# One loop over the chunks of a layer, with weight buffers chosen by a table, and the first chunk's weights split ahead of its rows

## The reference

```
gates = group_limited_router(x2d, w_router, router_bias)      # top 2 of 16 experts, weights sum to 1
for e in range(16):
    he = silu(x2d @ w_gate[e]) * (x2d @ w_up[e])              # 1024 -> 512
    y = y + gates[:, e:e+1] * (he @ w_down[e])                # 512 -> 1024
x = layer_norm(alpha * x + y)
```

## Time and profile before

| | us |
|---|---|
| median of 3 runs | 1079.57 (1076.26 to 1080.86) |
| the profiled execution | 1080.69 |
| its span, first to last instruction | 1078.9 |
| TensorE busy | 988.3 (92%) |
| VectorE, ScalarE, GpSimd busy | 808.8, 654.7, 546.2 |
| mean granted TensorE clock, 1 is full | 0.959 |
| HBM traffic over the span | 266 GB/s |

### The profile page before, as it was taken

How to read it: one execution, slowest core, us unless ns; L and a number is a source line. 1 busy time by engine, 2 the same in 40 slices (tenths; PEclk the granted TensorE clock), 3 DMA queues, 4 the chain that set the end, 5 groups by cost and what they waited for, 6 DMA issues and landing times.

```text
span 1078.9 us, 15494 instructions
## 1 busy us (share of the span) xinstructions
PE 988.3 (92%) x4852; PEld 793.1 (74%) x4852; DVE 808.8 (75%) x963; ACT 654.7 (61%) x733; POOL 546.2 (51%) x292
## 2 busy tenths in 40 slices
PE   5997999499999999999988988994999999999995
PEld 4875777377888788887667767783788888888882
DVE  2997757687878777777877977377777778787876
ACT  4324722367878787877513337412787878788861
POOL 3535354065656565645325364441556565656553
PEclk9999999689999999999989989996899999999998
DMA  8625183489999999994813211643899999999962
GB/s 287 198 78 204 40 299 137 138 312 349 359 346 363 360 338 340 346 360 158 259 41 107 89 48 40 228 181 125 289 366 349 376 358 356 367 353 335 366 226 84
DMA packets 122256, 268.51 MB, mean 249 GB/s; under 512 B 10475, under 2 KB 25995, under 8 KB 121712
## 3 DMA queue, kind: packets, MB, share of 16 engines
q1 hardware_dynamic: 111088, 247.14, 63.3%
q0 software_dynamic: 11136, 20.96, 7.3%
HBM read 259.19 MB, written 27.79 MB: 266 GB/s over the span
## 4 chain that ended last, share of the span: by engine, by line
PE 65%; DVE 22%; issue 4%; POOL 3%; DMA 2%; ACT 2%; DVEq 1%; SPq 0%; POOLq 0%; ACTq 0%
PE bank L763 32%; PE bank L781 17%; PE bank L424 7%; DVE bank L1155 7%; PE bank L741 2%; POOL xtok L1600 2%; PE bank L564 1%; DVE xTl L1124 1%; PE bank L735 1%; DVE moemem L1411 1%; DVE w_gate L1131 1%; DVE small L1119 1%; DMA w_gate<-in_w_in 1%; DMA y_rows<-moemem,scatter_idx 1%; DVE wl L1124 1%
## 5 line engine op out<-in xcount | busy, mean ns | idle before, releaser
L1649 POOL TENSOR_TENSOR wl<-w_down,wh 128x2048 fp32r<-128x2048 f32 x33 | 151.8, 4599 | 148.7 <-ACT wh L1023 148.7
L1124 DVE TENSOR_TENSOR wl<-w_gate,wh 128x2048 fp32r<-128x2048 f32 x71 | 166.8, 2349 | 48.3 <-ACT wh L1023 29.4
L1124 DVE TENSOR_TENSOR wl<-w_up,wh 128x2048 fp32r<-128x2048 f32 x66 | 151.2, 2293 | 29.5 <-ACT wh L1023 28.7
L1023 ACT ACTIVATE wh<-w_down 128x2048 fp32r<-128x2048 f32 x66 | 126.8, 1920 | 30.8 <-PE bank L763 30.2
L1023 ACT ACTIVATE wh<-w_up 128x2048 fp32r<-128x2048 f32 x66 | 126.5, 1917 | 31.0 <-PE bank L781 23.3
L763 PE MATMUL bank<-wh,xTl 128*128 128x512 f32 x528 | 144.0, 395 | 1.4 <-DVE xTl L1124 1.4
L763 PE MATMUL bank<-wl,xTh 128*128 128x512 f32 x528 | 143.6, 394 | 1.6 <-DVE wl L1124 1.6
L763 PE MATMUL bank<-wh,xTh 128*128 128x512 f32 x528 | 144.6, 397 | 0.2 <-ACT wh L1023 0.2
L1586 POOL TENSOR_TENSOR wl<-w_gate,wh 128x2048 fp32r<-128x2048 f32 x17 | 78.2, 4602 | 130.4 <-ACT wh L880 130.0
L1023 ACT ACTIVATE wh<-w_gate 128x2048 fp32r<-128x2048 f32 x66 | 126.5, 1917 | 11.0 <-PE bank L781 7.5
L1124 DVE TENSOR_TENSOR xTl<-bank,xTh 128x512 fp32r<-128x512 f32 (+1 forms) x168 | 89.6, 573 | 51.9 <-issue 24.7
(11 more groups left out here) (225 smaller groups left out, 1802.8 us busy)
## 6 DMA issues: line engine op xcount, KB each, us to landing
w_up<-in_exp_w_up SPq DMA_DIRECT2D x32, 2048.0 KB, 19.5
w_down<-in_exp_w_down SPq DMA_DIRECT2D x32, 2048.0 KB, 18.6
w_gate<-in_exp_w_gate SPq DMA_DIRECT2D x32, 2048.0 KB
w_gate<-in_w_in SPq DMA_DIRECT2D x14, 1024.0 KB, 5.4
w_gate<-in_w_out SPq DMA_DIRECT2D x8, 1024.0 KB, 5.0
y_rows<-moemem SPq DMA_DIRECT2D x8, 512.0 KB, 9.5
x_rows<-xtok POOLq DMA_DIRECT2D x8, 512.0 KB, 3.0
w_up<-y_rows SPq DMA_DIRECT2D x8, 512.0 KB, 5.0
```

The source lines that it names most:

```text
L1023: act.activation(wh[s][:, :], slot[r][p][:, cols], ACT.Copy).then_inc(half_high, 1)
L1124: return dve.tensor_tensor(out, src, high.bitcast(F32), ALU.subtract)
L1649: pool.tensor_tensor(wl[s][:, :], slot[r][p][:, cols], wh[s][:, :].bitcast(F32), ALU.subtract)\
```

## The change

1. *One loop.* The two sets of weight buffers become one tensor per piece of twice the length. VectorE writes three small tables (`loop_order`): for each chunk the buffer's offset (0 or 4096) and the count of landed loads at which its weights are there, and for each layer the last chunk's number. ScalarE, VectorE and GpSimd loop over the chunks once, reading the offset into a register. Chunk one of expert 0 stands ahead of the loop and the last chunk of expert 15 behind it.
2. *Landing semaphores.* One per piece instead of one per buffer. SP therefore waits, before each load, until the load before it in the same piece has landed.
3. *First chunk.* `begin_chunk` on ScalarE rounds halves 0, 1 and 2 ahead of the rows; VectorE subtracts half 0 between the slot tables and the token table, the gates come behind half 1, `loop_order` and `late_out` behind half 3. TensorE builds the late table within the chunk, between the gate halves and the up halves, and waits for `late_set` only ahead of the down halves. GpSimd waits for `late_set` at the end of its first chunk.
4. *Memory.* The mixing part's data in set 0 swap places between gate and up, so that SP loads gate of 0 early and up of 0 after `ln_out`; down of 1 is still behind `late_done`, gate of 2 is also behind `order_set`. The one-hot tables move out of `wh` and `wl`, the two tables in PSUM to banks 6 and 5.

```diff
-        slot = [[sb(f"w_{n}{r}", [P, 4096]) for n in ("gate", "up", "down")] for r in range(2)]
+        wexp = [sb(f"w_{n}", [P, 2 * 4096]) for n in ("gate", "up", "down")]
+        slot = [[w[:, 4096 * r:4096 * r + 4096] for w in wexp] for r in range(2)]
...
-        wexp_in = [[sem(f"{n}_in{r}") for n in ("gate", "up", "down")] for r in range(2)]
+        wexp_in = [sem(f"{n}_in") for n in ("gate", "up", "down")]
...
+        def half_from(piece, at, i):
+            return wexp[piece][:, bass.ds(at + 2048 * (i % 2), 2048)]
+        def half_start(eng, c):
+            return eng.value_load(half_at[0:1, bass.ds(c, 1)], min_val=0, max_val=4096)
... (SP)
-                load_expert(l, 0, 0, 1)
+                load_expert(l, 0, 0, 0)
                 sp.wait_ge(last_low, l + 1)
                 sp.wait_ge(piece_low, (PIECES - 1) * (l + 1))
+                sp.wait_ge(wexp_in[0], loads(l, 1))
                 load_expert(l, 1, 1, 0)
                 sp.wait_ge(ln_out, TT * (l + 1))
-                load_expert(l, 0, 0, 0)
+                load_expert(l, 0, 0, 1)
                 sp.wait_ge(late_done, l + 1)
+                sp.wait_ge(wexp_in[2], loads(l, 1))
                 load_expert(l, 1, 1, 2)
+                sp.wait_ge(order_set, l + 1)
                 with sp.Fori(1, E // 2) as pair:
                     for r in range(2):
                         e = 2 * pair + r
                         done = first_chunk(sp, l, e - 1)
+                        landed = sp.value_load(loads_of[0:1, bass.ds(done, 1)], ...)
                         for piece in range(3):
                             sp.wait_ge(split_done[piece], done)
+                            sp.wait_ge(wexp_in[piece], landed)
                             load_expert(l, e, r, piece)
... (TensorE)
                 widen(c, 0)
                 widen(c, 1)
+                if begins:
+                    late_tables(l)
                 pe.wait_ge(he_set, c + 1)
-                pe.wait_ge(late_set, l + 1)
                 widen(c, 2)
                 widen(c, 3)
...
-                pe.wait_ge(tab_set, l + 1)
                 for i in range(2):
                     turn_gathered(first, l, i)
-                late_tables(l)
-                with pe.Fori(first_chunk(pe, l, 0), first_chunk(pe, l, E)) as c:
+                chunk(l, first, True)
+                with pe.Fori(first + 1, first_chunk(pe, l, E)) as c:
                     chunk(l, c)
... (ScalarE)
+            def begin_chunk(l, c):
+                act.wait_ge(op_done, TT * (l + 1))
+                half_high_part(c, 0, src, loads(l, 1))
+                half_high_part(c, 1, src, loads(l, 1))
+                act.activation(idle[:, 1:2], eps, ACT.Silu)
+                half_high_part(c, 2, src, loads(l, 2))
+                act.sem_inc(heT_high, 2)
+                act.sem_inc(y_set, 1)
+                gathered_high(c, l, 0)
+                gathered_high(c, l, 1)
+                half_high_part(c, 3, src, loads(l, 2))
+                half_high_part(c, 4, src, loads(l, 1))
+                silu(c, l)
+                half_high_part(c, 5, src, loads(l, 1))
...
+                begin_chunk(l, first)
+                act.wait_ge(order_set, l + 1)
+                last = last_chunk(act, l)
+                with act.Fori(first + 1, last) as c:
+                    at = half_start(act, c)
+                    landed = act.value_load(loads_of[0:1, bass.ds(c, 1)], ...)
+                    chunk(l, c, lambda p, i: half_from(p, at, i), landed)
+                chunk(l, last, lambda p, i: half_of(p, 1, i), loads(l, E))
... (VectorE)
+            def loop_order(l):
+                c = cst[0:1, K_IOTA:K_IOTA + MAXCH].unsqueeze(2).broadcast_to([1, MAXCH, E - 1])
+                first = startf[0:1, l, 1:E].unsqueeze(1).broadcast_to([1, MAXCH, E - 1])
+                link(dve.tensor_tensor(later, c, first, ALU.is_ge))
+                link(dve.tensor_reduce(expert, later.bitcast(F32), AX.X, ALU.add))
+                dve.tensor_scalar(loads_of[:, :], expert, 16.0, float(loads(l, 1)), ALU.mult, ALU.add)
+                link(dve.tensor_copy(half_at[:, :], expert))
+                link(dve.tensor_scalar(half_at[:, :], half_at[:, :], 1, None, ALU.bitwise_and))
+                link(dve.tensor_scalar(half_at[:, :], half_at[:, :], 12, None, ALU.logical_shift_left))
+                link(dve.tensor_scalar(lasti[0:1, l:l + 1], starti[...], -1.0, None, ALU.add))
+                dve.sem_inc(order_set, 1)
...
+            def begin_chunk(l, c):
+                places(l)
+                half_low_part(c, 0, src)
+                tokens(l)
+                dve.sem_inc(heT_low, 2)
+                gathered_low(c, 0)
+                gathered_low(c, 1)
+                half_low_part(c, 1, src)
+                gates(l)
+                half_low_part(c, 2, src)
+                half_low_part(c, 3, src)
+                loop_order(l)
+                late_out(l)
+                half_low_part(c, 4, src)
+                hidden(c)
```

More of the change, by code:

```diff
@@ L235, in build @@
                              "lgT_done", "lgT_set"))
+        order_set = sem("order_set")
         idx_set, gathered, dst_set = sem("idx_set"), sem("gathered"), sem("dst_set")
@@ L256, in chunks_before, with last_chunk, loads, half_of @@
         def chunks_before(eng, l):
-            return first_chunk(eng, l - 1, E) if l > 0 else 0
-        def chunk_loops(eng, l, body):
-            with eng.Fori(0, E // 2) as pair:
-                starts = [first_chunk(eng, l, 2 * pair + r) for r in range(2)]
-                for r in range(2):
-                    if r == 1:
-                        starts.append(first_chunk(eng, l, 2 * pair + 2))
-                    with eng.Fori(starts[r], starts[r + 1]) as c:
-                        body(c, pair, r)
+            return eng.value_load(starti[0:1, bass.ds(l * (E + 1) - 1, 1)], min_val=E, max_val=MAXCH // 2) if l > 0 else 0
+        def last_chunk(eng, l):
+            return eng.value_load(lasti[0:1, bass.ds(l, 1)], min_val=E - 1, max_val=MAXCH - 2)
+        def loads(l, n):
+            return 16 * (E * l + n)
+        def half_of(piece, r, i):
+            return wexp[piece][:, 4096 * r + 2048 * (i % 2):4096 * r + 2048 * (i % 2) + 2048]
+        def half_from(piece, at, i):
+            return wexp[piece][:, bass.ds(at + 2048 * (i % 2), 2048)]
+        def half_start(eng, c):
+            return eng.value_load(half_at[0:1, bass.ds(c, 1)], min_val=0, max_val=4096)
         def turned(q, j, i):
@@ L334, in load_choices @@
                 sp.wait_ge(scattered, end * 16)
-                sp.wait_ge(split_done[1], last)
+                sp.wait_ge(split_done[0], last)
                 for j in range(TT):
@@ L784, in narrow, with chunk @@
                 mm.then_inc(half_used, 1)
-            def chunk(l, c):
+            def chunk(l, c, begins=False):
                 pe.wait_ge(sg_set, c + 1)
@@ L802, in chunk @@
                 turn_hidden(1)
+                if begins:
+                    pe.wait_ge(late_set, l + 1)
                 pe.wait_ge(y_set, c + (l + 1))
@@ L1079, in _ @@
                 act.activation(ex, lg, ACT.Exp).then_inc(rt_exp, 1)
-                act.activation(idle[:, 1:2], eps, ACT.Silu)
-                act.wait_ge(start_set, l + 1)
-                chunk_loops(act, l, lambda c, pair, r: chunk(l, c, pair, r))
-                end = first_chunk(act, l, E)
+                first = chunks_before(act, l)
+                begin_chunk(l, first)
[3 more added lines that the diff above has]
+                    at = half_start(act, c)
+                    landed = act.value_load(loads_of[0:1, bass.ds(c, 1)], min_val=16, max_val=16 * DEPTH * E)
+                    chunk(l, c, lambda p, i: half_from(p, at, i), landed)
+                chunk(l, last, lambda p, i: half_of(p, 1, i), loads(l, E))
+                end = last + 1
                 for i in range(2):
@@ L1546, in _ @@
                 route(l)
-                late_out(l)
-                chunk_loops(dve, l, lambda c, pair, r: chunk(l, c, pair, r))
-                end = first_chunk(dve, l, E)
+                first = chunks_before(dve, l)
+                begin_chunk(l, first)
+                last = last_chunk(dve, l)
+                with dve.Fori(first + 1, last) as c:
+                    at = half_start(dve, c)
+                    chunk(l, c, lambda p, i: half_from(p, at, i))
+                chunk(l, last, lambda p, i: half_of(p, 1, i))
+                end = last + 1
                 for i in range(2):
@@ L1637, in scatter, with chunk @@
                                         bounds_check=T - 1, oob_is_err=False, compute_op=ALU.add).then_inc(scattered, 16)
-            def chunk(l, c, r):
+            def chunk(l, c, src, begins=False):
                 pool.wait_ge(xg_turned, c * 2 + 2 * (l + 1))
@@ L1708, in _ @@
                 pool.wait_ge(tab_set, l + 1)
-                pool.wait_ge(late_set, l + 1)
```

(8 more changed lines are left out.)

114 lines of the change are left out of this document (67 added, 47 removed).

## The result

The changed kernel takes 1090.44 us (median of 4 runs, 1090.2 to 1091.36), the kernel before 1079.17 us beside it; the ratio of the kernels is 1.0086, 95% interval [1.0059, 1.0112] (the medians alone give 1.0104). It is slower, by about twice the forecast of 4.6 us. The profiled executions have spans of 1078.9 and 1088.4 us, 9.5 apart.

A forecast was written before the change was run, and what follows sets the result against it. TensorE and the weights stream were both taken as full, the stream deciding at the layer ends. Layer terms of +2.4 and +2.2 gave +4.6 us on 1080.69: 1085.3, as a median 1084; range 1073 to 1092.

The forecast's parts named there:

- rival C: SP's wait for the landed load starves the full weights stream: 8.2 us added to the forecast, 1092; chance 0.14.
- `w_down` of expert 1 later by 5.9 and 6.1: First chunk, SP: this load waits for the late table, now behind the gate halves; issued 5.9 (layer 0), 6.1 us later.
- Order table 2.8 us, ends 1.4 and 5: First chunk, VectorE: two 720-element operations at 0.9 us each plus five small ones, 2.8 us; bounds 1.4 and 5.
- hidden product earlier by 4.2 and 2: First chunk: hidden product at 225.0 instead of 229.19, 4.2 us earlier in layer 0; gain about 2 in layer 1.
- Stream ends 2.4 and 3.7 later: Weights loads: more idle DMA time ahead of the full stretch ends the stream 2.4 (layer 0), 3.7 us (layer 1) later.
- The end follows the stream, +2.4 and +2.2: Layer ends: the late stream sets them, +2.4 us in layer 0 without slack, +2.2 in layer 1 after 1.5 slack.
- Rival D: Loop's start: the first chunk isn't earlier while the late table moves toward 221; +8 us, 1088; chance 0.10.
- Gain given back to the stream where it is the bound: Layer ends: TensorE's gains of 3.5 and 2 us from the first chunk are given back as waits for weights.
- In the loop 0: Loop chunks: one head per chunk and the table reads cost 0 us; 6 us if ScalarE's cover is gone.
- Cap 0: SP's wait for the landed load caps the queue at three loads; nothing runs dry, so it costs nothing.
- B: Full stream: a deeper queue wastes DMA time, so the cap of three loads gains; 1077 or 1073 us; chance 0.24.
- E: Whole expert part: TensorE is the bound after all, gains of 3.5 and 2 us stand; 1073 us; chance 0.10.

The follow-up runs named there:

- e7: Changed kernel loading only the first quarter of `w_down` of experts 2 to 15, so the stream is light; 1084.78 us, ratio 1.0024 to the kernel before.
- e5: Kernel before, with SP waiting ahead of each looped expert load until the load before it of the same piece has landed; 1080.45 us, ratio 0.9984.
- e10: Kernel before, with `w_down` of expert 1 waiting for VectorE's last gate operation instead of TensorE's late table; 1082.48 us, ratio 1.0018.
- e8: Kernel before, loading only the first quarter of `w_down` of experts 2 to 15; 1079.56 us, ratio 0.9973.
- e4: Changed kernel with loops per expert, no order table and no wait for the landed load, weights still ahead of the rows; 1077.67 us, ratio 0.9964 to before.
- e6: e4 with `w_down` of expert 1 waiting for VectorE's last gate operation instead of TensorE's late table; 1074.33 us, ratio 0.9928 to the kernel before.
- e11: e6 with the second half of `w_down` of expert 1 loaded right behind `w_up` of expert 0; 1069.51 us, ratio 0.990 to the kernel before.

## Why the prediction came out as it did

It named the side (slower, for the loss in the first chunk's stream and the gain given back) and half the size. That its range takes in the measured time is luck: 1090 is above the forecast's own 1079 to 1089 and reached only by the price of rival C, which didn't happen, and the likeliest class it gave was a change of under 0.5%. Step by step, in us from the first tokens:

- *First product earlier by 2.6*: 3.0 and 2.3. *Clock at the upper level by 216*: mean 0.86 in 211 to 217, and 1.00 from 213 on. By the times of the kernel before that is 210, 2 us sooner than the earliest rise that I had, 212. *Halves 2 and 3 done at 219.6*, which is +18.4: +18.0. These steps held.
- *`w_down` of expert 1 later by 5.9 and 6.1*: 4.8 and 5.8. Held, a little high. In layer 0 it is the lower end that I had given: with the clock up early, the late table starts as soon as the gates are ready (at +13.6; forecast +13.7). The upper bound of the next step for layer 1 should have been 7.7 and not 7; nothing hangs on it.
- *Order table 2.8 us, ends 1.4 and 5*: from 222.40 to 229.09, 6.7 us. **This is the step that failed.** I priced its small operations by VectorE's own rows, as if nothing but their size counted, and took the ends of the range from the same reasoning. The rest of the term is right: without the wait it is 6.7 - 4.15 + 0.2 = 2.7. The wait for GpSimd's subtraction was no term of the sum, though that subtraction stands in the profile right beside the hidden product, and the 2.05 us of GpSimd's copy in the same trace were a sign of such waits. Even the upper end was too low.
- What hung on it: *order table at 222.4* (+21.2) was +24.8; *`w_gate` of expert 2 later by 2.2* was 7.8 and 9.2, with 2 us from the table's end to the issue; *hidden product earlier by 4.2 and 2* was 0.7 earlier and 2.0 later.
- A term that was missing: TensorE's clock falls in its idle stretch of 7.12 us, and the second chunk takes 1.95 and 2.6 us more. By estimate the clock is most of that: in layer 0 it was at 0.50 for some 4.4 us of work (from 232.09 to about 236.5, by the stretches), and half of it is 2.2.
- *Stream ends 2.4 and 3.7 later*: 4.0 and 7.7. *The end follows the stream, +2.4 and +2.2*: +4.2 and +4.9. In layer 0 most of that is the stream (e7: the last hidden product at +320.5, 5.5 us earlier, when it is light). In layer 1 it is not: there the periods from the third chunk to the one before the last are 18.20, light or not, and the +4.6 stand already at the second chunk (with some chance in it: with the same first chunk as before, the first hidden product of layer 1 comes at +25.2 in e5 and e10, +27.7 in e8). Rival D's outcome (nothing won in front), by another mechanism.
- *Gain given back to the stream where it is the bound*: shown by e4, and supported by e6 against e4 in layer 1 and by e11 in layer 0.
- *In the loop 0*: held; periods of 18.20 in the one loop, 18.20 in the nested ones.
- *Cap 0*: held (e5). B and C are out. E is out for layer 0; in layer 1 TensorE does run at 18.20 almost to the end, but there was no gain in front to keep.
- Expected and seen: `w_up` landing capped near 20 us, and ScalarE waiting in many of the last chunks (11 and 5 against 5 and 0).

## What to carry to other kernels

Before an operation is priced by its size, look at what GpSimd does at that moment: 48 elements cost 4.15 us behind a subtraction of 128x2048, and when one operation is freed of the wait the next one that needs the port takes it over. Order tables and the like belong where GpSimd has nothing long under way, or in no place at all (loops per expert cost nothing here). And where weights are waited for at the end, a gain at the head of a layer lasts only if the weights start earlier too: with both (e11), the version without table is 1.0% faster than before.

## What the runs showed that I had not expected

The blocked operation shows as busy, not as idle: 4.15 us of "work" for 48 elements, with no releaser beside it. A mean far above its neighbours' in the groups (2947 ns beside 169 for the same shape) is the sign. And one idle stretch of 7 us of TensorE cost nearly 2 more behind it (20.15 instead of 18.20), in which the work began at a clock of 0.50.
